# Eight of the 22 hidden tiles of two FFN down projections, from plain products to seven products of 256 columns

## The reference, cut to what matters

```
def swiglu_ffn(h, w_in, w_out):                       # the first block
    gate, up = jnp.split(h @ w_in, 2, axis=-1)
    return (jax.nn.silu(gate) * up) @ w_out

x = x + swiglu_ffn(rms_norm(x, norm_ffn_g), w_ffn_in, w_ffn_out)        # "fa" in the kernel
x = rms_norm(x, norm_final_g)
x = x + 0.5 * swiglu(rms_norm_2(x, ffn1_norm), ffn1_gate, ffn1_up, ffn1_down)   # "fb"
...  # second mixer, cross attention
x = x + 0.5 * swiglu(rms_norm_2(x, ffn2_norm), ffn2_gate, ffn2_up, ffn2_down)   # "fc"
```

## Time and profile before

| | us |
|---|---|
| median of 3 runs | 2385.22 |
| the profiled execution | 2385.45 |
| its span, first to last instruction | 2383.6 |
| TensorE busy in it | 2359.7 |

### The profile page before, as it was taken

How to read it: one execution, slowest core, us unless ns; L and a number is a source line. 1 busy time by engine, 2 the same in 40 slices (tenths; PEclk the granted TensorE clock), 3 DMA queues, 4 the chain that set the end, 5 groups by cost and what they waited for, 6 DMA issues and landing times.

```text
span 2383.6 us, 34351 instructions
## 1 busy us (share of the span) xinstructions
PE 2359.7 (99%) x13792; PEld 2007.5 (84%) x13792; DVE 1525.4 (64%) x2207; ACT 1167.8 (49%) x1910; POOL 266.8 (11%) x210
## 2 busy tenths in 40 slices
PE   8999999999999999999999999999999999999998
PEld 7777778777888888899988899988887888899987
DVE  5688746468775465687743687753677565777742
ACT  7766664234464254455543555532644354555532
POOL 0000000455200010110002200001033201100000
PEclk9999999999999999999999999999999999999999
DMA  6221234333576231233233243233322232333231
GB/s 199 78 72 51 82 107 161 105 98 104 164 223 217 97 124 62 89 124 107 89 107 97 62 131 102 87 110 94 105 69 63 91 112 74 103 110 107 95 99 55
DMA packets 171119, 251.89 MB, mean 106 GB/s; under 512 B 9936, under 2 KB 89040, under 8 KB 170960
## 3 DMA queue, kind: packets, MB, share of 16 engines
q1 hardware_dynamic: 169808, 248.13, 32.8%
q10 hardware_dynamic: 1152, 1.57, 0.2%
HBM read 231.83 MB, written 16.78 MB: 104 GB/s over the span
## 4 chain that ended last, share of the span: by engine, by line
PE 95%; DVE 3%; ACT 1%; issue 1%; DMA 0%; POOL 0%; SPq 0%; DVEq 0%; POOLq 0%; ACTq 0%
PE bank L1349 93%; PE bank L1509 1%; DVE wlo L2314 1%; PE bank L1532 0%; DVE T L2322 0%; PE bank L1633 0%; PE bank L1657 0%; DMA zb<-scr_z 0%; DVE macc L2314 0%; PE bank L1475 0%; ACT whi L1751 0%; DMA raw<-in_w_in 0%; DVE ml L2322 0%; DVE xg L2318 0%; DVE bank L2620 0%
## 5 line engine op out<-in xcount | busy, mean ns | idle before, releaser
L2314 DVE TENSOR_TENSOR wlo<-raw,whi 128x1024 fp32r<-128x1024 f32 (+2 forms) x310 | 381.6, 1234 | 244.0 <-ACT whi L1751 243.9
L1349 PE MATMUL bank<-xopr,shi 128*128 128x256 f32 x2688 | 484.1, 283 | 0.1
L1751 ACT ACTIVATE whi<-raw 128x1024 fp32r<-128x1024 f32 (+2 forms) x310 | 318.7, 1034 | 281.2 <-PE bank L1349 274.4
L1349 PEld LDWEIGHTS bank<-xopr,shi 128*128 128x128 f32 x2688 | 419.5, 192 | 0.5 <-DVE slo L2314 0.3
L1349 PE MATMUL bank<-xh,whi 128*128 128x512 f32 x1016 | 411.5, 405 | 8.2 <-DVE wlo L2314 8.2
L1349 PE MATMUL bank<-xh,wlo 128*128 128x512 f32 x1016 | 397.9, 392 | 0.0
L1349 PE MATMUL bank<-xl,whi 128*128 128x512 f32 x1016 | 397.2, 391 | 0.0
L1349 PE MATMUL bank<-xopr,slo 128*128 128x256 f32 x1344 | 380.3, 283 | 0.0
L1349 PEld LDWEIGHTS bank<-xopr,slo 128*128 128x128 f32 x1344 | 258.0, 192 | 0.0
L1349 PEld LDWEIGHTS bank<-xh,whi 128*128 128x128 f32 x1016 | 191.5, 188 | 64.7 <-issue 20.2
L1349 PEld LDWEIGHTS bank<-xh,wlo 128*128 128x128 f32 x1016 | 191.3, 188 | 41.7
(11 more groups left out here) (380 smaller groups left out, 4230.8 us busy)
## 6 DMA issues: line engine op xcount, KB each, us to landing
raw<-in_w_in SPq DMA_DIRECT2D x92, 512.0 KB, 3.6
raw<-in_ffn_down SPq DMA_DIRECT2D x44, 512.0 KB, 3.8
quarter<-in_w_ffn_in SPq DMA_DIRECT2D x32, 512.0 KB, 4.5
quarter<-in_ffn_gate SPq DMA_DIRECT2D x32, 512.0 KB, 3.9
quarter<-in_ffn_up SPq DMA_DIRECT2D x32, 512.0 KB, 4.8
raw<-in_w_ffn_out SPq DMA_DIRECT2D x22, 512.0 KB, 3.8
raw<-in_w_xattn_kv SPq DMA_DIRECT2D x16, 512.0 KB, 4.2
raw<-in_w_kv_mem SPq DMA_DIRECT2D x16, 512.0 KB, 4.9
```

Of the source, the lines that this page charges most:

```text
L1349: return e.matmul(out, l, r, start=start, stop=stop, skip_group_check=skip)
L1751: return e.activation(out, in_, ACT.Copy)
L2314: return e.tensor_tensor(out, a, b, op)
```

## The change

It sets `BACKED = ("fa", "fb")`. For these two FFNs the way back takes the hidden tiles 8 to 21 in plain slots (7 slots per group instead of 11), and tiles 0 to 7 after them in two rounds of seven products, numbered as pairs 12 and 13 (512 output features each). `fc` stays as it is.

```
+        BACKED = ("fa", "fb",)
+        BEHIND = [(12, 1), (12, 5), (12, 6), (12, 2), (12, 7), (13, 1), (12, 4), (13, 5), (12, 3), (13, 6), (13, 2),
+                  (13, 7), (13, 3), (13, 4)]
...
-                weights(f"{tag}d{i}", columns(down, i), 22, "h" + tag)
+                weights(f"{tag}d{i}", columns(down, i), 22, "h" + tag, order=range(8, 22, 2) if tag in BACKED else None)
+            if tag in BACKED:
+                BACK[tag], SOURCE["b" + tag] = len(slots), io[down]
+                slots.extend((None, x) for x in BEHIND)
```

```
+        def back_operands(tag):
+            for kp in range(4):
+                step("back_hi", tag, kp, 0)      # ACT: copies of 256 and 512
+                step("back_sum", tag, kp)        # DVE: 512, 256, 256, each waiting for the last
+                yield
+                step("back_lo", tag, kp, 0)      # DVE: 256 and 512
+                step("back_hi", tag, kp, 1)      # ACT: 1024
+                yield
+                step("back_lo", tag, kp, 1)      # DVE: 1024
+                yield
+                split_h(tag, 14 + 2 * kp)
+                yield
+                split_h(tag, 15 + 2 * kp)
...
+            if tag in BACKED:
+                split_h(tag, 12)
+                soon(1, split_h, tag, 13)
+                behind = start(back_operands(tag), 5.0)
...
+                gemm(f"{tag}d0", lambda m: step("residual", out, m, "part"))
+                drain(behind)
+                gemm(f"{tag}d1", lambda m: step("residual", out, 4 + m, "part"), hook=begin_back(tag))
+                back(tag, out)
+                return
```

(The comments on engines and sizes are added here.) `begin_back` issues the four loads of weight quarters (two DMAs of 512 KB each) at the start of the second group and prepares the first products from its tile 23 of 28 on. `back` runs the 14 products. Their results are added to the residual by `back_add`, four per pair, each over two tiles and 256 tokens:

```
+        def back(tag, out):
+            for n, (i, p) in enumerate(BEHIND):
...
+                step("product", tag, i, p)
+                pay()
+                owed.append(lambda i=i, p=p: back_finished(tag, out, i, p))
+                point()
+                prepare_sum(tag, n + 4, BEHIND)
+                prepare_last(tag, n + 6, BEHIND)
+                prepare_hi(tag, n + 3, BEHIND)
+                if n == 10:
+                    ORDER.append(("mark", (f"{tag}b",)))
+                if n in (10, 12, 13):
+                    tile_ready(out, max(0, n - 11))          # x_split, x_lo one point later
+                if 9 <= n < 13:
+                    squares(out, n - 9)                      # twice for the norms of fb
+                if n in (11, 13):
+                    split_to(first + n // 2 - 4)             # the next projection's slots
+            pay()
+            settle()
+            split_to(first + 3)
+            for x, k in enumerate((3, 4, 6, 5, 7)):
+                tile_ready(out, k)
+                point()
+                if x:
+                    soon(x - 1, squares, out, k)
+        def back_finished(tag, out, i, p):
+            if p == 1:         step("seed_b", tag, i)
+            elif p in (5, 6):  step("keep", tag, i, p)
+            elif p == 2:       step("back_add", tag, out, i, 11)
+            elif p == 7:       step("seed_f", tag, i); step("c22", tag, i); soon(0, "back_add", tag, out, i, 22)
+            elif p == 4:       step("back_add", tag, out, i, 21)
+            elif p == 3:       step("c12", tag, i); soon(0, "back_add", tag, out, i, 12)
```

More of the change, by code:

```diff
@@ new lines, in begin_back, with hook @@
+        def begin_back(tag):
+            def hook(n):
+                if n == 0:
+                    for i in (12, 13):
+                        for e in range(2):
+                            step("quarter", tag, i, e)
+                if n in (23, 25, 27):
+                    prepare_hi(tag, (n - 23) // 2, BEHIND)
+                if n in (24, 26):
+                    prepare_sum(tag, n // 2 - 11, BEHIND)
+            return hook
+        def back_finished(tag, out, i, p):
+            if p == 1:
+                step("seed_b", tag, i)
+            elif p in (5, 6):
+                step("keep", tag, i, p)
+            elif p == 2:
+                step("back_add", tag, out, i, 11)
+            elif p == 7:
+                step("seed_f", tag, i)
+                step("c22", tag, i)
+                soon(0, "back_add", tag, out, i, 22)
+            elif p == 4:
+                step("back_add", tag, out, i, 21)
+            elif p == 3:
+                step("c12", tag, i)
+                soon(0, "back_add", tag, out, i, 12)
@@ new lines, in tile_ready, with squares @@
+        def tile_ready(out, k):
+            step("x_split", out, k)
+            soon(0, "x_lo", out, k)
+        def squares(out, k):
+            square(out, k)
+            if out == "fb":
+                square("fb2", k)
+        def back(tag, out):
+            first = BACK[tag] + len(BEHIND)
+            ready[0] = loaded[0] = first
+            upto[0] = stop_after(first)
+            for n, (i, p) in enumerate(BEHIND):
+                if p == 1:
+                    for b, letter in enumerate("aebf"):
+                        seven_ring(i)[0].new(letter, tag, i, among=(b,))
+                    for b, what in enumerate(("c22", "u2")):
+                        tmp2.new(what, tag, i, among=(b + 2 * (i % 2),))
+                step("product", tag, i, p)
+                pay()
[20 more added lines that the diff above has]
+                    soon(x - 1, squares, out, k)
@@ L1106, in build @@
             def build():
-                built.append(start(operands(tag), 3))
+                built.append(start(operands(tag), 4 if tag == "fb" and "fa" in BACKED else 3))
             if tag == "fb":
@@ L1124, in both @@
                         soon(3, scale)
-                    soon(3, both)
-                later(2, first)
+                    soon(2 if "fa" in BACKED else 3, both)
+                later(4 if "fa" in BACKED else 2, first)
             else:
@@ L1154, in build @@
         ffn("fb", "mix2")
-        later(1, norm("mix2"))
+        later(4 if "fb" in BACKED else 1, norm("mix2"))
         step("mark", "mixer2")
-        step("bounds")
+        soon(7 if "fb" in BACKED else 0, "bounds")
         def ev_f(m):
@@ new lines, in back_lo @@
+            def back_lo(tag, kp, part):
+                t, tr, h = xop[kp], xopr[kp], four[kp]
+                w.wait_ge(*at("op hi", "b" + tag, kp, part))
+                if part == 0:
+                    tt(tr[:, 4, :], h[:, 0, :], tr[:, 11, :].bitcast(F32), ALU.subtract)
+                    ins = tt(tr[:, 5:7, :], h[:, 2:4, :], tr[:, 12:14, :].bitcast(F32), ALU.subtract)
+                else:
+                    ins = tt(tr[:, 0:4, :], t[:, 0:4, :], tr[:, 7:11, :].bitcast(F32), ALU.subtract)
+                ins.then_inc(*up("x_lo", ("op lo", "b" + tag, kp, part)))
@@ L2858, in w_sum @@
                 else:
[L2859 removed]
+                    there = slot_of(tag, i, 5 if i in (10, 13) else 2)
                     w.wait_ge(*at("w hi", there))
```

232 lines of the change are left out of this document (171 added, 61 removed).

## The result

The changed kernel takes 2388.92 us (median of 22 runs, 2386.39 to 2390.77), the one before 2385.55 (22 runs, 2384.03 to 2386.96): a ratio of 1.0013, 95% interval 1.0008 to 1.0019. The forecast was 2379.8 with a range up to 2383.2, and the prediction's own sum of every hole at its upper end was 2384.4. It was wrong.

What follows compares the result with a forecast made beforehand. TensorE, busy 2359.7 us with 95% of the chain, was taken as the bound. 2385.45 - 6.4 + 0.5 + 0.1 + 0.2 + 0.1 + 0.1 = 2380.0, stated as 2379.8 for the runs' median; range 2378.4 to 2383.2.

Steps and rivals of the forecast that it cites:

- every hole at its upper end: Slow end of the forecast: holes of 0.9, 0.2, 1 and 0.5 us, first group 1.5 us late twice: 2384.4.
- TensorE's own work: Each way back: 43.5 us of plain matmuls go, 40.3 us of products come; saves 3.2 us, 6.4 for both.
- rival 3: Spacing of 256-column matmuls worse than in the sevens: no gain at 129.5 ns, 2427 us at 192 ns; chance 0.01.
- The first plain group: Way back's first plain slots, most crowded for DVE: nothing late, but thin, with 1 to 2 us of margin.
- cost 0: Second plain group: quarter loads in SP's queue stand before no urgent load, so TensorE does not wait.
- The hand-over in fa: End of fa's 14 products, start of next projection: TensorE waits 0 to 0.9 us for seed and low parts; 0.5 taken.
- the norm behind it: Partition sums nine output tiles after fa's products wait 0 to 1 us for POOL's and DVE's sums; 0.2 taken.
- rival 1: Holes at two or three seams take half the gain: 2382.0 us; chance 0.24.
- rival 2: DVE's waits on ACT make the first plain group late: 5.4 us slower, 2390.6, at 1.8 us per pair; chance 0.06.
- the prediction's own measure of 4.8 us: A difference under 0.2%, 4.8 us, counts as none; chances were faster 0.65, same 0.29, slower 0.06.
- rivals 1 and 4: Besides rival 1: plain work not taken away, or another engine paces later stages; 2385 us, chance 0.04.
- The moved scaling: Eight DVE instructions of 0.75 us, 6.0 us in all, enter fb's seven: cost 0 to 0.5 us, 0.1 taken.

Runs made afterwards that it cites:

- the last run: The reordered kernel with pair 13's quarter loads issued after the second plain group's fifth output tile instead of its first: 2380.37 us, 0.9976.
- the reordered kernel: Changed kernel, DVE summing fb's squares of tiles 2 to 6 (POOL tile 1), steps reordered, first slot split earlier, partition sums one tile later: 2380.63 us, 0.9980.
- fa alone: Kernel before with only fa's way back changed, fb's left as it was: 2391.91 us, 1.0025.
- the two kernels without the last hole: Changed kernel with fb's partition sums one output tile later (2386.16 us), or with six throwaway matmuls before that wait (2387.46 us).

## Why the prediction was wrong, step by step

**TensorE's own work: right.** 3.2 us per way back were worked out; 3.1 came in fb, and 3.0 in fa with the hole of 0.3 at its end taken off. The load-bound spacing of rival 3 did not show.

**The first plain group: no hole, and the margin was not thin.** No hole stands in either. DVE is busy 29.42 of its first 32.93 us, against 19.82 of 32.65. The text had the last low part at 1231.1 and 1 to 2 us to spare; it ended at 1226.60, 5.2 us before the seventh slot (1199.17 + 32.64).

```profile
1199.17:1232.10 32.93, 32.93 (x148) 27.26 (x147) 29.42 (x45) 19.31 (x30) 0.00 (x0) 1.00 0.38 120
```
```profile
1225.31 1.29 DVE L2472 TENSOR_TENSOR hl<-hid,hh 128x512 fp32r<-128x512 f32 x2
```

**SP's queue: the step "cost 0" failed by a little.** I wrote that the loads behind the quarters "need the same slots split". The last plain slot's load could have gone out before them: in the last run it does. In the profiles it cost 0 to 0.8 us, 0 in that of the changed kernel.

**"The hand-over in fa", 0.5 us, and "the norm behind it", 0.2 us, are the steps that failed.** Measured, they are 0.3 us at the end of the way back and 9.0 behind it. The place and its queues were right: first split late by 0.3, `xl` of tile 1 late by 0.7, both in the text's order. The price was mis-sized, though its row was read: I applied the 1.55 us of an `xl` beside POOL to one instruction, the next one wanted, and let every later step run at its price alone. With T, the end of the 14th product, at 1315.8, the change has POOL adding from T-7 (1308.55) to T+16 (1332.01), with one rest of 2.5 us, over seven of the eight `xl`, the adds from SBUF tiles and two splits. These seven `xl` took about 1.78 us each, which is 7 us more by itself, and POOL's sums, at 1.29 in my sum, mostly 1.74 to 2.27. So tiles 3 and 5 and the last sum came late as well, in places for which the text has no hole.

**The holes' own price and the clock had no term.** The five holes in the third row (0.73, 0.05, 1.57, 1.43 and 0.44 us) are 4.2 us by the profile. Here a hole costs more than its row says: before the one of 0.73 us, matmuls start at 1316.68 and then 1317.81 and 1318.15, 1.47 us for two steps of 0.227, 1.0 lost.

```profile
1316.68 0.40 PE L1481 MATMUL bank<-xh,wlo 128*128 128x512 f32 x1
1317.81 0.50 PE L1481 MATMUL bank<-xh,whi 128*128 128x512 f32 x1 [0.73 <-DVE xl L2480]
1318.15 0.39 PE L1481 MATMUL bank<-xl,whi 128*128 128x512 f32 x1
```

The holes of 0.05 and 1.57 us lose 0.27 more in the same way. With 0.28 more for each of five holes, an estimate, that is 1.4 us; 4.2, 1.4 and the clock's 3.1 are 8.7 of the 9.0. Of the rivals, none was this one: rival 1 had the holes but at half the gain, rival 2 looked for the slow side in the first plain group. By the prediction's own measure of 4.8 us the result is "same", which had 0.29, but for rivals 1 and 4 and a part of rival 2; no chance stood for what came.

**The moved scaling: right.** fb's seven is 161.27 us with DVE at 129.14, 0.4 less than before. The 0.4 to 0.5 us at `ACT R`, where a spread bank is read late, is in every kernel with fa's way back changed and had no term.

## What to carry to other kernels

Before moving work so that two engines overlap more, list for each instruction of the longer queue whether its price is that of running alone or beside the other engine, and price the whole queue at the second. A stretch where an in-order engine has no idle time at all is where a gain can be lost, but the order decides: DVE has none in the reordered kernel either (1307.3 to 1332.0), and TensorE waits for it nowhere there. So order the steps by when they are wanted, and give the shared work to the engine that does it in 0.6 us and not the one that does it in 1.3 and stops the other. And where TensorE's holes come close together, as the 1.57 and 1.43 us here, count the clock with them.

## What the runs showed of the hardware

**DVE and POOL take turns.** Beside POOL's sums of two SBUF tiles, DVE's instructions with two SBUF inputs are longer by at most about the same amount: 0.74 to 1.78, 0.68 to 1.77, 1.21 to 2.31, that is 1.04 to 1.10 us, whatever their length, near one POOL sum (1.29). Some lose only part of it (an add of two SBUF tiles at 1.27, a `wlo` at 1.72). With a PSUM input they are not longer (0.68). The Trainium skill (SBUF — State Buffer, section "SBUF: two separate sides") states this: the two engines hold a port pair in turn, exclusively, for a whole instruction, and a DVE instruction with two SBUF inputs contends only with a POOL one that reads SBUF. The trace agrees: no stretched instruction loses more than one POOL sum takes. I had read the row and not the rule, which says that it holds for every such instruction.

**Holes and the clock.** Two idle stretches of 1.57 and 1.43 us with 1.0 us of work between them were followed by the lower clock for 6.8 us (with fa alone after 1.53 and 1.43, for over 6); with the second filled or gone, the 1.57 us and others before it were not, nor was one hole of 2.0 us, or one of 1.1. Each of these is one profile. The other executions go the same way: the mean clock is 0.996 or 0.997 in 15 of the 22 of the changed kernel, and in none of the 22 of the two kernels without the last hole (medians 2386.16 and 2387.46). A mean of 0.998 says nothing of this place: the profile of the kernel before has it too, with 1.00 here. After the hole of 2.0 us two of eleven executions have 0.997, so there the clock may have fallen at times.
